# Token rows of a layer kernel laid out on 1024-byte multiples, and two early expert blocks turned into split products

## What is computed

```python
def peer_ffn(h, peer_wq, sub_keys1, sub_keys2, peer_u, peer_v):
    q = (h @ peer_wq).reshape(B, T, PEER_HEADS, PEER_QDIM)      # 8 heads of 256
    s1, s2 = (q halves against the 128 sub-keys of each half)
    v1, i1 = lax.top_k(s1, 16)
    v2, i2 = lax.top_k(s2, 16)
    # best 16 of the 256 sums, softmax over them, expert number = i1 * 128 + i2
    ...
    a = jnp.einsum('td,tkd->tk', hb, peer_u[eb])
    a = jax.nn.gelu(a, approximate=False)
    return jnp.einsum('tk,tkd->td', (gb * a), peer_v[eb])
```

## Time and profile before

| | |
|---|---|
| median of three runs | 958.64 us |
| the profiled execution, as a run | 957.38 us |
| its span in the profile | 955.6 us |
| TensorE busy | 948.3 us (99%) |
| VectorE, ScalarE, GpSimd busy | 753.0, 468.7, 209.6 us |
| granted TensorE clock | 1.00 all through |
| first early block to the picks' turning | 153.8 to 236.3 us |
| gate products | 242.0 to 344.9 us |
| early down products, main loop | from 347.9 us, from 444 us to the end |

### The profile page before, as it was taken

How to read it: one execution, slowest core, us unless ns; L and a number is a source line. 1 busy time by engine, 2 the same in 40 slices (tenths; PEclk the granted TensorE clock), 3 DMA queues, 4 the chain that set the end, 5 groups by cost and what they waited for, 6 DMA issues and landing times.

```text
span 955.6 us, 16376 instructions
## 1 busy us (share of the span) xinstructions
PE 948.3 (99%) x5324; PEld 829.7 (87%) x5324; DVE 753.0 (79%) x1453; ACT 468.7 (49%) x849; POOL 209.6 (22%) x249
## 2 busy tenths in 40 slices
PE   9999999999999999999999999999999999999998
PEld 9998899998999987888888888888888888888887
DVE  6899759998999988888677777767767767767766
ACT  6576554423899963344344344344344344344342
POOL 3075138886777720000000000000000000000000
PEclk9999999999999999999999999999999999999999
DMA  9544138726544468776665666666666666665664
GB/s 296 150 133 133 45 115 283 206 78 211 148 140 130 138 204 243 239 239 231 199 192 183 196 188 186 196 188 186 194 187 190 195 186 188 194 188 188 192 188 147
DMA packets 73593, 174.72 MB, mean 183 GB/s; under 512 B 6208, under 2 KB 39104, under 8 KB 73296
## 3 DMA queue, kind: packets, MB, share of 16 engines
q1 hardware_dynamic: 73120, 172.02, 58.2%
q0 software_dynamic: 288, 2.10, 1.1%
q10 hardware_dynamic: 144, 0.08, 0.0%
HBM read 165.26 MB, written 6.82 MB: 180 GB/s over the span
## 4 chain that ended last, share of the span: by engine, by line
PE 93%; ACT 3%; DVE 2%; DMA 2%; issue 0%; SPq 0%; POOL 0%; POOLq 0%; DVEq 0%; ACTq 0%
PE psum L1996 35%; PE psum L1976 17%; PE psum L1861 11%; PE psum L1979 9%; PE psum L1561 5%; PE psum L1830 4%; PE psum L1939 3%; PE psum L1577 2%; DMA rr<-big 1%; PE psum L1618 1%; PE psum L1739 1%; PE psum L1822 1%; PE psum L1855 1%; ACT rr L788 1%; DMA gel<-up_kept 1%; PE psum L1605 0%
## 5 line engine op out<-in xcount | busy, mean ns | idle before, releaser
L1996 PE MATMUL psum<-rr 128*128 128x512 f32 x1536 | 366.4, 391 | 0.2 <-DVE rr L1311 0.2
L1996 PEld LDWEIGHTS psum<-rr 128*128 128x128 f32 x1536 | 287.5, 188 | 60.4 <-DVE rr L1311 0.8
L1976 PE MATMUL psum<-h_all,rr 128*128 128x512 f32 x728 | 260.6, 392 | 0.0
L815 ACT ACTIVATE rr<-raw 128x1024 fp32r<-128x1024 f32 x94 | 99.7, 1061 | 295.7 <-PE psum L1996 294.5
L1279 DVE TENSOR_TENSOR rr<-raw,rr 128x1024 fp32r<-128x1024 f32 x94 | 115.2, 1225 | 125.2 <-ACT rr L815 125.2
L1979 PE MATMUL psum<-h_all,rr 128*128 128x256 f32 x728 | 188.7, 280 | 0.0
L1976 PEld LDWEIGHTS psum<-h_all,rr 128*128 128x128 f32 x728 | 136.6, 188 | 26.9
L1979 PEld LDWEIGHTS psum<-h_all,rr 128*128 128x128 f32 x728 | 136.7, 188 | 7.2
L1861 PE MATMUL psum<-t32s,raw 128*128 128x256 f32 x576 | 131.4, 379 | 0.0
L1861 PEld LDWEIGHTS psum<-t32s,raw 128*128 128x128 f32 x576 | 106.3, 190 | 12.7
L1193 DVE TENSOR_TENSOR rr<-raw,rr 128x1024 fp32r<-128x1024 f32 x90 | 109.8, 1220 | 1.4 <-ACT rr L704 1.4
(11 more groups left out here) (215 smaller groups left out, 1125.6 us busy)
## 6 DMA issues: line engine op xcount, KB each, us to landing
raw<-in_peer_v_dram SPq DMA_DIRECT2D x128, 512.0 KB, 3.5
raw<-in_peer_u_dram SPq DMA_DIRECT2D x127, 512.0 KB, 3.7
big<-in_w_in_dram SPq DMA_DIRECT2D x10, 1024.0 KB, 6.0
big<-in_peer_wq_dram SPq DMA_DIRECT2D x8, 1024.0 KB, 6.6
up_kept<-gel SPq DMA_DIRECT2D x36, 128.0 KB, 3.8
gel<-up_kept SPq DMA_DIRECT2D x34, 128.0 KB, 3.7
big<-in_w_out_dram SPq DMA_DIRECT2D x4, 1024.0 KB, 5.2
rr<-big POOLq DMA_DIRECT2D x2, 1024.0 KB, 9.8
```

The costliest lines, as they stand in the source:

```text
L815: act.activation(v_sp[s][:, 0, :], v_raw[s], ACT.Copy).then_inc(v_hi, 1)
L1976: return pe.matmul(both, ut[s][:, 0, k, :], ht[:, :, k, :], start=(k == 0), stop=(k == DK - 1))
L1996: i = pe.matmul(psum[:, 4 + 2 * t + n, :], g_sp[:, s, x, t * P:(t + 1) * P], v_sp[s][:, y, n * 512:(n + 1) * 512], start=(first and m == 0 ...
```

## The change

1. **Token rows.** The split token rows of the expert part (not those of the attention part) move to a new view `hs` of the same array: for each channel group 256 high columns and right behind them 256 low columns, each row on a multiple of 1024 bytes. The high parts of the picks stand behind it in one piece (`p_high`). All uses in the first up, the loop's `high` and `low`, and the copies that write the parts are rewritten for it.
2. **Two split blocks.** Early blocks 13 and 14 (`SPLIT_E`), the one just ahead of the picks' turning and the one just behind it, become split products of 24 matmuls. Each needs a high part of its weights from ScalarE (`early_high`) and a low part of 1024 elements from GpSimd.
3. **Fillers.** `PRE` is 13 in place of 12: five matmuls of block 15 stand in front of the first gate product, where four stood.
4. **Waits.** The gated columns of the second group wait for block 14's product, whose operands lie in the same place. The wait for the tokens' low parts moves from behind the gate products to block 13.

```diff
-PRE, TAIL = 12, 0
+PRE, TAIL = 13, 0
 EXP_AT = EARLY_TOP - 5
+SPLIT_E = (FILL0 - 1, FILL0)
...
+        h_flat = h_all[:, :, :, :].rearrange("p a k t -> p (a k t)")
+        hs = h_flat[:, 0:2 * DK * SEQ].rearrange("p (k a t) -> p a k t", a=2, k=DK)
+        p_high = h_flat[:, 2 * DK * SEQ:2 * DK * SEQ + SEQ]
...
+        early_sp = [rr[:, n:n + 2 * D].rearrange("p (a k n) -> p a k n", a=2, k=DK) for n in (2 * D, 4 * D)]
...
         def p_hi(tok, n):
-            return hm[:, tok // P, tok % P // META, tok % META:tok % META + n]
+            return p_high[:, tok:tok + n]
...
+            def early_high(n):
+                e = SPLIT_E[n]
+                act.wait_ge(ld_t[e % 3], 16 * (e // 3 + 1))
+                act.activation(early_sp[n][:, 0], u_ring[e % 3].rearrange("p (k n) -> p k n", k=DK), ACT.Copy).then_inc(eu_hi, 1)
...
             for e in range(EXP_AT + 1, EARLY_TOP - 2):
+                if e == EARLY_TOP - 4:
+                    early_high(0)
                 early_gelu(e)
                 if e == EARLY_TOP - 4:
                     act.wait_ge(ld_uf, 16)
                     act.activation(ut[0][:, 0], u_first, ACT.Copy).then_inc(ut_hi, 1)
+            early_high(1)
...
             for n in range(1, N_OUT):
                 low_part(n)
+            for n, e in enumerate(SPLIT_E):
+                pool.wait_ge(eu_hi, n + 1)
+                pool.tensor_tensor(early_sp[n][:, 1], u_ring[e % 3].rearrange("p (k n) -> p k n", k=DK), f(early_sp[n][:, 0]), ALU.subtract)\
+                    .then_inc(eu_lo, 1)
...
+                    if q == 1 and not part:
+                        pool.wait_ge(e_up, SPLIT_E[1] + 1)
...
-            e = EARLY_TOP - 2
-            pe.wait_ge(ld_t[e % 3], 16 * (e // 3 + 1))
-            pe.wait_ge(e_gel, e - 1)
-            early_part(e, 0, DK).then_inc(e_up, 1)
+            def early_split(n):
+                e = SPLIT_E[n]
+                for a, b in ((0, 0), (0, 1), (1, 0)):
+                    if (a, b) == (0, 0):
+                        pe.wait_ge(eu_hi, n + 1)
+                        pe.wait_ge(a_hi, 4)
+                    elif b:
+                        pe.wait_ge(p_hlo, N_OUT)
+                    else:
+                        pe.wait_ge(eu_lo, n + 1)
+                    for k in range(DK):
+                        i = pe.matmul(psum[:, early_bank(e), 0:SEQ], early_sp[n][:, a, k, :], hs[:, b, k, :],
+                                      start=(a + b + k == 0), stop=(a == 1 and k == DK - 1))
+                i.then_inc(e_up, 1)
+
+            pe.wait_ge(e_gel, EARLY_TOP - 3)
+            early_split(0)
             pe.wait_ge(d_pick, PH + 1)
...
                     e, k = FILL0 + n // DK, n % DK
+                    if e == SPLIT_E[1]:
+                        if k == 0:
+                            early_split(1)
+                        continue
...
-            pe.wait_ge(p_hlo, N_OUT)
...
                 def high(k):
-                    return pe.matmul(both, ut[s][:, 0, k, :], ht[:, :, k, :], start=(k == 0), stop=(k == DK - 1))
+                    return pe.matmul(both, ut[s][:, 0, k, :], hs[:, :, k, :], start=(k == 0), stop=(k == DK - 1))
```

More of the change, by code:

```diff
@@ L787, in gated @@
                             act.wait_ge(d_plo, 1)
+                        if q == 1 and j == GRP - ACT_T and not part:
+                            act.wait_ge(e_up, SPLIT_E[1] + 1)
                         i = act.activation(pairs_at[q % 2][:, j, part, :], cols[q % 2][:, j - ACT_T, :, 1], ACT.Copy, scale=scale)
@@ L1265, in _ @@
                     dve.wait_ge(pk_ev, 3)
-                    dve.tensor_tensor(picks[:, 2, :].rearrange("p (a k m) -> p a k m", a=2, k=DK),
-                                      psum[:, 7, 0:SEQ].rearrange("p (a k m) -> p a k m", a=2, k=DK), f(hm), ALU.subtract)\
-                       .then_inc(d_plo, 1)
+                    dve.tensor_tensor(picks[:, 2, :], psum[:, 7, 0:SEQ], f(p_high), ALU.subtract).then_inc(d_plo, 1)
                 if q >= RS:
@@ L1961, in _ @@
                 fill(fill_end(q - 1), fill_end(q))
-            pe.wait_ge(p_hlo, N_OUT)
             def first_up(s, b):
                 pe.wait_ge(ut_lo, b + 1 - EARLY)
-                product(psum[:, 2 * s, 0:SEQ], lambda a, k: ut[s][:, a, k, :], lambda b, k: ht[:, b, k, :], a_done)
+                product(psum[:, 2 * s, 0:SEQ], lambda a, k: ut[s][:, a, k, :], lambda b, k: hs[:, b, k, :], a_done)
             def up(s, b):
@@ L1975, in high @@
                 def high(k):
-                    return pe.matmul(both, ut[s][:, 0, k, :], ht[:, :, k, :], start=(k == 0), stop=(k == DK - 1))
+                    return pe.matmul(both, ut[s][:, 0, k, :], hs[:, :, k, :], start=(k == 0), stop=(k == DK - 1))
                 def low(k):
-                    pe.matmul(both[:, 0, :], ut[s][:, 1, k, :], ht[:, 0, k, :], start=False, stop=False)
+                    pe.matmul(both[:, 0, :], ut[s][:, 1, k, :], hs[:, 0, k, :], start=False, stop=False)
                 high(0)
```

8 lines of the change are left out of this document (4 added, 4 removed).

## The result

The changed kernel is slower: 966.36 us, the median of 12 runs (960.48 to 967.21), against 958.12 for the kernel before on the same chip (12 runs, 957.10 to 959.58). The ratio is 1.0069, with a 95% interval of 1.0058 to 1.0079. My forecast was 960.0 with a range of 956.3 to 961.4. The time is outside it, and on the side to which I gave a chance of 0.18.

A forecast was written before the change was run, and what follows sets the result against it. TensorE, busy 99%, was taken as the bound. With the token rows at 0, the first gate product came +1.7 us later, less the filler's 0.37: +1.35, so 958.64 goes to 960.0, range 956.3 to 961.4.

The forecast's parts named there:

- the zero for the token rows: Main loop, high products: the rows' new place changes nothing, 0 us, with bounds of 0.9 us over 91 blocks.
- the one timing for which the sum was made: Picks' turning: VectorE's steps before `d_pick` begin at 231.33, GpSimd's subtractions delay them, and `d_pick` comes at 238.2, not 233.8.
- Nothing later is tied to an absolute time: Behind the gates: the early down products and the loop simply follow the shift, total +1.35 us.
- the median 1.26 above the profiled run: Whole kernel: the median stands 1.26 us above the profiled execution, so 958.7 profiled means 958.64 before and 960.0 after.
- Rival (c): Loop: one-run reads of high products meet another reader or writer, all eight take 0.24; +8 us, 968; chance 0.1.
- rival E: Loop, set up in the follow-up experiments: aligned rows meet accesses of VectorE, ScalarE or the DMAs; no chance given.
- the sign that the pace is not fixed: Start of a loop block: what follows a high product starts 0.24 us behind it, against 0.229 on average.
- Rival (b): Loop's up part: the rows' new place makes products faster, some 0.04 us a block, 1.8 to 3.6 us; chance 0.15.
- The collision: Before the picks' turning: GpSimd's two subtractions hold VectorE's steps, first gate product +1.7 us; chance 0.5 as summed.
- the filler's give-back: Gate stretch: one six-filler group falls to five, 3.54 to 3.17 us, giving 0.37 us back.
- the third case of rival (a): Picks' turning: L1236 slips in before GpSimd's second subtraction, block 36's low part waits; +0.3 us; chance of (a) 0.25.
- The split work: Early blocks 13 and 14: 2.84 us split in place of 3.45 plain, removing 0.62 us twice.

The follow-up runs named there:

- the split blocks' profile: Two split blocks, PRE 13 and the waits, token rows in their old place, against the kernel before: 961.68 us, ratio 1.0033; profiled run 962.98.

## Why the prediction was wrong, by its steps

Two steps failed, and each alone, put on top of my 960.0, would have left the range: the zero for the token rows (+3.0) and the one timing for which the sum was made (+5.0 in the median).

- **The token rows' new place, 0 with bounds of 0.9 us: wrong, +3.0.** I inferred from an equal 0.118 for aligned and old rows that the place costs nothing, and found the same 0.229 for the high product on the old rows and for the down product. Neither row is a high product on the new rows: the first is a product of 256 columns, in which the stationary operand lies elsewhere too, and the second has other operands and neighbours. The pace turned out to depend on both. Measured, the high product goes from 0.2296 to 0.2350, 8 x 91 times: 3.9 us, of which the up's low products and the down part give some back. The bound of 0.01 us a block was the rounding of my rows, not a bound on the effect.
- **"Nothing later is tied to an absolute time", and the median 1.26 above the profiled run: wrong, and the larger miss.** The sum was made for one timing of the picks' chain, that of the one profile. The other comes in 10 of 18 runs of the changed kernel, with an eleventh between the levels, and adds 5 to 6 us: the late chain, which the slack of 2.5 us had mostly hidden, and the clock that falls in the longer wait. With it the median goes from 961.5 to 966.4.
- **Rival (c)** had the right side and the wrong mechanism and size: the high products do slow down, by 0.005 us, but not by meeting a reader (rival E fell), nor to 0.24 throughout; +3.0 in place of +8. I named the sign that the pace is not fixed, and then gave it 0.1.
- **Rival (b)**, that the aligned rows help: the opposite of what happened.
- **The collision: right, and in size.** VectorE's first cast took 2.45 us and ended at 233.86 (it was to wait until 233.5), the last step at 235.63 (235.6), the turning at 238.20 (238.2), the first gate product at 243.75 (243.7), the filler's give-back 0.36 (0.37). The rule of the Trainium skill (SBUF — State Buffer, "Who interferes with whom") with the earlier trace rows gave it before the run. At the loop it was +1.04, where I had +1.35. It is not the only order: the second profile of the changed kernel had the third case of rival (a), with the loop 0.50 late.
- **The split work: about right.** 2.95 us from block 14's start to block 15's, 2.84 forecast. On the old rows it was 2.91 (the version with one split block), so 0.04 can be the rows' place.

The sum by what was measured: 957.4 (profiled run before) + 3.0 + 1.0 = 961.4, against 961.45. For the other timing, the split blocks' profile gives 3.3 for the turning and 1.3 behind it: 966.0, against a median of 966.36.

## What to carry to other kernels

What is multiplied by the number of blocks needs its zero shown at the precision that the product asks for. Here 91 blocks made 3 us of 33 ns. The starts of the real sequence of matmuls with the new places would have been wanted, not the mean of another sequence. Before giving an idle engine work, look for the slack of the chain that shares its port, not only in the profiled execution but at the latest that this chain ever comes; a late transfer far ahead uses it up. Put such work behind the last step of that chain. And a longer array moves those behind it: look up where they lie before a shift is called the only edit.

## What the runs showed of the hardware that I had not expected

- TensorE's pace depends on where its operands lie, with nothing else running: 24 F32R products of 512 columns took from 5.44 to 5.64 us by start and step of the moving rows alone, those of 256 columns 0.118 or 0.120 each. Rows on multiples of 1024 bytes (from the array's start) had the longest block of the layouts in this loop, with two others, though not in the streams. One piece or two made no difference.
- The weights' place counts as well: 64 bytes off alone, a stream took 0.233 a matmul in place of 0.227; with the rows moved by the same 64 bytes it was 0.227 again, and in the loop up and down parts repeated this.
- The matmuls before count too: the down part changed from 2.735 to 2.758 us with unchanged operands. No rule that I have fits all eight layouts.
- In a wait of TensorE of 3.2 to 3.5 us the granted clock fell to 0.50 for 3.4 us (two profiles); in one of 2.14 us it did not.
- One load of 1 MB took 8.3 to 8.4 us in eleven profiles and 11.1 to 12.2 in six. Where GpSimd's work had used up the slack of VectorE's chain behind it, the two profiles with the late load were of the upper level of their kernels' times.
